# A two-layer block on one core: feed-forward gate and up with weights stationary, both parts of the tokens as 512 moving columns, and another order of weight tiles

## The reference

```python
D_MODEL = 2048; SEQ = 256; D_FF = 5632; FFN_CONV_WIDTH = 3

def causal_dwconv(u, w, b):      # K taps over positions, w[K-1] hits the current token
    up = jnp.pad(u, ((0, 0), (K - 1, 0), (0, 0)))
    return b + sum(up[:, k:k + S] * w[k] for k in range(K))

def conv_glu_ffn(h, w_gate, w_up, conv_w, conv_b, w_down):
    g = causal_dwconv(h @ w_gate, conv_w, conv_b)
    return (jax.nn.silu(g) * (h @ w_up)) @ w_down

h = rmsnorm(x, g_ffn[l]) * (1.0 + sc2) + sh2
x = x + gt2 * conv_glu_ffn(h, w_ffn_gate[l], w_ffn_up[l], ffn_conv_w[l], ffn_conv_b[l], w_ffn_down[l])
```

## Time and profile before

| | |
|---|---|
| median of 3 runs | 3034.95 us (3034.37 to 3036.27) |
| span of the profiled execution | 3033.7 us (no other time is given for it) |
| TensorE matmuls | 3020.3 us busy, 14581 instructions |
| TensorE weight loads (beside the matmuls) | 2537.3 us busy |
| VectorE, ScalarE | 1971.3 us, 1494.1 us busy |
| from memory | 658.21 MB, 217 GB/s in the mean |

### The profile page before, as it was taken

How to read it: one execution, slowest core, us unless ns; L and a number is a source line. 1 busy time by engine, 2 the same in 40 slices (tenths; PEclk the granted TensorE clock), 3 DMA queues, 4 the chain that set the end, 5 groups by cost and what they waited for, 6 DMA issues and landing times.

```text
span 3033.7 us, 38889 instructions
## 1 busy us (share of the span) xinstructions
PE 3020.3 (100%) x14581; PEld 2537.3 (84%) x14581; DVE 1971.3 (65%) x2081; ACT 1494.1 (49%) x1798; POOL 15.1 (0%) x32
## 2 busy tenths in 40 slices
PE   9999999999999999999999999999999999999999
PEld 7899878888888888888888888888888888888887
DVE  7999997866655568665555656565475555566564
ACT  6555456444444545554444444545454444444543
POOL 0000000000000000000000000000000000000000
PEclk9999999999999999999999999999999999999999
DMA  9998998865556556555555455555555555455555
GB/s 397 414 403 297 360 344 299 303 220 188 188 187 190 189 180 227 172 177 179 190 177 194 160 173 194 174 183 186 163 177 180 194 173 194 165 170 189 169 183 173
DMA packets 167272, 658.21 MB, mean 217 GB/s; under 512 B 18593, under 2 KB 18913, under 8 KB 154721
## 3 DMA queue, kind: packets, MB, share of 16 engines
q1 hardware_dynamic: 163264, 634.53, 60.6%
q0 software_dynamic: 3584, 21.48, 1.9%
q10 hardware_dynamic: 290, 0.33, 0.0%
HBM read 654.14 MB, written 2.11 MB: 216 GB/s over the span
## 4 chain that ended last, share of the span: by engine, by line
PE 91%; DVE 5%; DMA 3%; ACT 1%; issue 0%; SPq 0%; DVEq 0%; ACTq 0%
PE pg L1229 27%; PE pg L1231 27%; PE pg L1230 27%; DMA w_raw<-w 2%; DVE w_lo L1891 2%; PE pm L1264 1%; DVE R L1835 1%; PE pm L1292 1%; PE pm L1722 1%; DMA R<-w_ada 1%; PE pg L1315 1%; PE pg L1316 1%; PE pg L1317 1%; DVE x_rows L1835 1%; PE pm L1616 0%
## 5 line engine op out<-in xcount | busy, mean ns | idle before, releaser
L1771 DVE TENSOR_TENSOR w_lo<-w_raw,w_hi 128x1024 fp32r<-128x1024 f32 x868 | 1060.9, 1225 | 948.5 <-ACT w_hi L625 944.2
L625 ACT ACTIVATE w_hi<-w_raw 128x1024 fp32r<-128x1024 f32 x868 | 919.8, 1060 | 1295.6 <-PE pg L1231 1285.9
L1229 PE MATMUL pg<-w_hi,hT_hi 128*128 128x512 f32 x2912 | 1144.2, 393 | 1.0 <-DVE w_lo L1891 0.7
L1231 PE MATMUL pg<-w_hi,hT_lo 128*128 128x512 f32 x2912 | 1134.1, 389 | 0.0
L1230 PE MATMUL pg<-w_lo,hT_hi 128*128 128x512 f32 x2912 | 1133.5, 389 | 0.0
L1229 PEld LDWEIGHTS pg<-w_hi,hT_hi 128*128 128x128 f32 x2912 | 547.0, 188 | 114.4 <-issue 3.4
L1231 PEld LDWEIGHTS pg<-w_hi,hT_lo 128*128 128x128 f32 x2912 | 546.6, 188 | 114.5
L1230 PEld LDWEIGHTS pg<-w_lo,hT_hi 128*128 128x128 f32 x2912 | 547.1, 188 | 110.0
L1229 PE MATMUL pg<-w_hi,y_parts 128*128 128x512 f32 x864 | 337.6, 391 | 0.0
L1231 PE MATMUL pg<-w_hi,y_parts 128*128 128x512 f32 x864 | 336.4, 389 | 0.0
L1230 PE MATMUL pg<-w_lo,y_parts 128*128 128x512 f32 x864 | 336.1, 389 | 0.0
(11 more groups left out here) (321 smaller groups left out, 1957.4 us busy)
## 6 DMA issues: line engine op xcount, KB each, us to landing
w_raw<-w SPq DMA_DIRECT2D x1008, 512.0 KB, 4.1
R<-w_ada SPq DMA_DIRECT2D x59, 1024.0 KB, 8.6
x_rows<-w_ada SPq DMA_DIRECT2D x18, 1024.0 KB, 10.6
R<-w_ada POOLq DMA_DIRECT2D x11, 1024.0 KB, 7.9
R<-w SPq DMA_DIRECT2D x16, 512.0 KB, 9.4
R<-w_ada SPq DMA_DIRECT2D x10, 512.0 KB, 7.5
R<-mem_T SPq DMA_DIRECT2D x8, 512.0 KB, 9.2
x_rows<-x SPq DMA_DIRECT2D x4, 1024.0 KB, 9.3
```

The costliest lines, as they stand in the source:

```text
L625: act.activation(w_hi[:, g % RING, :, :].rearrange("p c n -> p (c n)"), raw[:, g % RING, :], ACT.Copy).then_inc(hi_done, 1)
L1229: pe.matmul(out, hi, w_hi[:, slot, c, :], start=start, stop=False)
L1231: return pe.matmul(out, lo, w_hi[:, slot, c, :], start=False, stop=stop)
L1771: tt(flat(w_lo[:, g % RING, :, :]), raw[:, g % RING, :], flat(w_hi[:, g % RING, :, :]).bitcast(F32), ALU.subtract).then_inc(lo_done, 1)
```

## The change

- Gate and up in the blocks: `both_parts` takes the place of `group`. 128 columns of a weight tile are stationary, and the result has channels on partitions, so that there is nothing to transpose. The high and the low part of the tokens lie in one tensor, `hT_parts`, and move side by side as 2 x 256 columns against the high weights; the low weights meet the high part alone, 256 columns, into the first half of the same bank. The four pieces of 128 channels fill the four banks of `pm`.
- The halves of each bank are added by VectorE in one reduction (`summed`), to `g_sum` or `u_sum`. The tap and the convolution read `g_sum`, the product reads `u_sum`. `take`, `g_tok`, `u_tok` and `ff_T` are gone.
- Order of tiles in a step: gate of j + 1 (8), the first two down pieces of j (4), up of j + 1 (8), the other two down pieces (4). The stream of weights is laid out accordingly.
- Gate and up of block 0, in the front, go by `column_passes`. ScalarE takes `g0` in four activations with the tap's bias and scale; `u0` is read from PSUM by VectorE. Tap, convolution and Silu of block j + 1 are made in step j.
- Each engine's order is written anew (`block_of` on VectorE). The 16 `weigh` pieces are spread over three blocks. The load of the final gain waits for `aT_ready` in place of `ff_ps`.

```diff
-COLUMNS = ("y", "q0", "x", "k0", "q1", "k1")
+COLUMNS = ("y", "q0", "x", "k0", "q1", "k1", "g0", "u0")
...
-F_ACTS = list(itertools.accumulate(int(not name.startswith("o")) for name in FRONT))
+F_ACTS = list(itertools.accumulate(int(not name.startswith("o") and name != "u0") for name in FRONT))
...
-        hT_hi = sb("hT_hi", [P, KD, S], F32R)
-        hT_lo = sb("hT_lo", [P, KD, S], F32R)
+        hT_parts = sb("hT_parts", [P, 2, KD, S], F32R)
+        hT_hi, hT_lo = hT_parts[:, 0, :, :], hT_parts[:, 1, :, :]
...
-        g_tok = view(24, TB, NW)
-        u_tok = view(28, TB, NW)
+        g_sum = view(24, 4, S)
+        u_sum = view(28, 4, S)
...
-                    pool.wait_ge(ff_ps, NFF * 4)
+                    pool.wait_ge(aT_ready, NFF)
...
-                        if name == "x":
+                        if name in ("x", "g0"):
+                            taps, w, bias = (4, "conv_w", "conv_b") if name == "x" else (3, "ffn_w", "ffn_b")
                             for b in range(4):
-                                i = act.activation(X_[:, b, :], front_bank(u)[:, b // 2, b % 2 * S:(b % 2 + 1) * S],
-                                                   ACT.Identity, bias=V("conv_b")[:, b:b + 1],
-                                                   scale=V("conv_w")[:, 4 * b + 3:4 * b + 4])
+                                i = act.activation(front_dest[name][:, b, :],
+                                                   front_bank(u)[:, b // 2, b % 2 * S:(b % 2 + 1) * S],
+                                                   ACT.Identity, bias=V(bias)[:, b:b + 1],
+                                                   scale=V(w)[:, taps * b + taps - 1:taps * b + taps])
...
-                for q in range(2):
-                    act.wait_ge(ff_ps, j * 4 + q + 1)
-                    for c in range(2):
-                        k = 2 * q + c
-                        i = act.activation(g_cv[:, k, :], pm[q][:, c * S:(c + 1) * S], ACT.Identity,
-                                           bias=ff_col("ffn_b", j, k, 1), scale=ff_col("ffn_w", j, k, 3, 2))
-                    i.then_inc(ff_tap, 1)
+                act.wait_ge(ff_summed, 2 * j)
+                for k in range(4):
+                    i = act.activation(g_cv[:, k, :], g_sum[:, k, :], ACT.Identity,
+                                       bias=ff_col("ffn_b", j, k, 1), scale=ff_col("ffn_w", j, k, 3, 2))
+                i.then_inc(ff_tap, 1)
...
+            silu(0)
             with act.Fori(0, NFF - 2) as j:
                 g0 = G_FF + 2 + j * 3
-                advance(g0)
-                tap(j)
-                act.wait_ge(ff_ps, j * 4 + 4)
-                take(g0, 0, flat(g_tok))
-                split(g0 + 1, range(4, 6))
-                silu(j)
-                split(g0 + 1, range(6, 8))
-                split(g0 + 2, range(4))
-                take(g0 + 1, 1, flat(u_tok))
-                advance(g0 + 2)
+                split(g0, range(4, 13))
+                tap(j + 1)
+                split(g0, range(13, 19))
+                silu(j + 1)
+                split(g0, range(19, 28))
...
+            split(g0, range(4, 13))
+            tap(j + 1)
+            split(g0, range(13, 14))
             act.wait_ge(y_ready, 2)
             gate_row(1)
-            split(g0 + 2, range(4, 6))
-            tap(NFF - 1)
-            split(g0 + 2, range(6, 8))
-            silu(NFF - 1)
-            split(g0 + 3, range(8))
+            split(g0, range(14, 19))
+            silu(j + 1)
+            split(g0, range(19, 32))
...
+            def both_parts(G, first):
+                for j in range(GT):
+                    g = first + j
+                    pe.wait_ge(lo_done, G * GT + g + 1)
+                    for c in range(KC):
+                        k = j * KC + c
+                        for b in range(4):
+                            hi, lo = (w[:, g % RING, c, b * P:(b + 1) * P] for w in (w_hi, w_lo))
+                            pe.matmul(pm[b].rearrange("p (a s) -> p a s", a=2), hi, hT_parts[:, :, k, :],
+                                      start=k == 0, stop=False)
+                            i = pe.matmul(pm[b][:, 0:S], lo, hT_hi[:, k, :], start=False, stop=k == KD - 1)
+                    i.then_inc(tile_used, 1)
...
-            def ff_T(j):
-                pe.wait_ge(evac_act, A_FF + j * 2 + 2)
-                transposes(g_tok, (0, 1), ff_ps)
-                transposes(u_tok, (2, 3), ff_ps)
...
+            def down(G, j, n, first, lhs, between=lambda i: None):
+                pe.wait_ge(evac_dve, V_FF + j * NB + n - 1)
+                short(G, first, n, lhs, between)
             with pe.Fori(0, NFF - 2) as j:
                 g0 = G_FF + 2 + j * 3
-                pe.wait_ge(evac_act, A_FF + j * 2 + 1)
-                pe.wait_ge(evac_dve, V_FF + j * NB - 1)
-                group(g0, 0, hT)
-                ff_T(j)
-                pe.wait_ge(evac_dve, V_FF + j * NB)
-                group(g0 + 1, 1, hT)
-                down(g0 + 2, j, A_FF + j * 2 + 4)
+                pe.wait_ge(ff_summed, 2 * j + 1)
+                both_parts(g0, 0)
+                pe.wait_ge(aT_ready, j + 1)
+                for n in range(2):
+                    down(g0, j, n, 8 + 2 * n, (aT_hi, aT_lo))
+                pe.wait_ge(ff_summed, 2 * j + 2)
+                both_parts(g0, 12)
+                for n in range(2, 4):
+                    down(g0, j, n, 16 + 2 * n, (aT_hi, aT_lo))
             j = NFF - 2
             g0 = G_FF + 2 + j * 3
-            pe.wait_ge(evac_act, A_FF + j * 2 + 1)
-            pe.wait_ge(evac_dve, V_FF + j * NB - 1)
-            group(g0, 0, hT)
-            ff_T(j)
-            pe.wait_ge(evac_dve, V_FF + j * NB)
-            group(g0 + 1, 1, hT)
+            pe.wait_ge(ff_summed, 2 * j + 1)
+            both_parts(g0, 0)
+            down(g0, j, 0, 8, (aT_hi, aT_lo))
+            pe.wait_ge(ff_summed, 2 * j + 2)
+            pe.wait_ge(ff_tap, j + 1)
             gate_row(1)
-            for n in range(NB):
-                pe.wait_ge(evac_dve, V_FF + j * NB + n - 1)
-                pe.wait_ge(evac_act, A_FF + j * 2 + (3 if n == 0 else 4))
-                short(g0 + 2, n, (aT_hi, aT_lo))
-                if n == 0:
-                    pe.wait_ge(gate_sb, 2)
-                    ff_T(NFF - 1)
+            down(g0, j, 1, 10, (aT_hi, aT_lo))
+            pe.wait_ge(gate_sb, 2)
+            both_parts(g0, 12)
+            for n in range(2, 4):
+                down(g0, j, n, 16 + 2 * n, (aT_hi, aT_lo))
...
+            def conv(j, k, src):
+                d = 2 - k
+                for m in range(4):
+                    w = vec[:, bass.ds(VEC["ffn_w"][0] + (j * 4 + m) * 3 + k, 1)]
+                    step(stt(g_cv[:, m, d:], src(m)[:, 0:S - d], w, g_cv[:, m, d:], ALU.mult, ALU.add))
+                step.settle()
+            def convolved(j, k):
+                if k == 1:
+                    dve.wait_ge(ff_tap, j)
+                conv(j, k, lambda m: g_sum[:, m, :])
+                if k == 0:
+                    dve.sem_inc(ff_conv, 1)
+            def summed(G, last, dest):
+                dve.wait_ge(tile_used, G * GT + last)
+                dve.tensor_reduce(out=dest, in_=pm_all[:, :, :].rearrange("p b (a s) -> p b s a", a=2), op=ALU.add,
+                                  axis=mybir.AxisListType.X).then_inc(ff_summed, 1)
+            def product(j):
                 dve.wait_ge(ff_silu, j + 1)
-                dve.wait_ge(ff_ps, j * 4 + 4)
-                for q in range(2):
-                    step(tt(flat(a_f[:, 2 * q:2 * q + 2, :]), flat(g_cv[:, 2 * q:2 * q + 2, :]), pm[2 + q][:, :],
-                            ALU.mult))
+                if isinstance(j, int) and j == 0:
+                    dve.wait_ge(tile_used, FT)
+                    for q in range(2):
+                        step(tt(flat(a_f[:, 2 * q:2 * q + 2, :]), flat(g_cv[:, 2 * q:2 * q + 2, :]), pg[1][:, q, :],
+                                ALU.mult))
+                else:
+                    u = u_sum
+                    dve.wait_ge(ff_summed, 2 * j + 1)
+                    step(tt(flat(a_f), flat(g_cv), flat(u), ALU.mult))
                 step.settle()
-                split_act(a_f, hi, lo, aT_ready)
-            def down_out(G, j, n):
-                dve.wait_ge(tile_used, G * GT + 2 * n + 2)
+            def product_high(hi):
+                step(dve.tensor_copy(hi, a_f))
...
+            def block_of(j, weighed=(), final=False):
                 g0 = G_FF + 2 + j * 3
+                def to(first, last):
+                    for g in range(first, last):
+                        split(g0, (g,))
+                        if g in weighed:
+                            weigh(next(gate_blocks))
+                to(4, 5)
                 product(j)
+                to(5, 6)
+                dve.wait_ge(tile_used, g0 * GT)
+                product_high(aT_hi)
+                to(6, 7)
+                product_low(aT_hi, aT_lo)
```

(37 more changed lines are left out.)

## The result

| | before | with the change |
|---|---|---|
| median of 21 runs | 3035.07 us (3033.06 to 3038.2) | 3039.39 us (3036.82 to 3042.41) |
| ratio | 1 | 1.0013, 95% interval 1.0007 to 1.0019 |
| span of the profiled execution | 3033.7 us | 3035.4 us (its time 3037.19) |

The change makes the kernel slower by 0.13%, 4.3 us (2.1 to 5.8 by the interval). The forecast was 3.8 us faster, in a range of 3022 to 3040 that the median is inside of. The sign was wrong.

What follows compares the result with a forecast made beforehand. TensorE's own sequence of matmuls was taken to bound the kernel. Terms -19.5 + 8.3 + 2.5 + 0.7 + 1.5 + 1.6 + 0.9 + 0.2 made -3.8 us: 3031 us, range 3022 to 3040.

Steps and rivals of the forecast that it cites:

- transposes and restarts: TensorE in the blocks: removing 176 transposes and the slow restarts behind them, 11 sets of 1.77 us, saves 19.5 us.
- gate and up in the blocks, 1280 pairs: TensorE, 160 tiles: 8 matmuls of 512 columns and 8 of 256 replace 12 of 512, adding 8.3 us.
- wait at the entry: TensorE before block 0's first group waits for VectorE's signal after a low part: +1.5 us with the cold restart.
- wait at the gate row: Last block: the gate row's transpose waits for the tap of block 10, +1.6 us (0.5 to 3.7).
- wait for down's bank: Last block: down of block 10 waits for the bank VectorE empties for n = 2, +0.9 us (0 to 3.0).
- the steady rates: TensorE's matmul prices inside long runs of one form: 0.2267 us for 512 columns, 0.1198 us for 256.
- Alternating is dear: Rival, chance 0.13: two-run operands or each change of form cost TensorE extra; at 0.354 us a pair, 3041 us.
- Short behind long is cheap: Rival, chance 0.20: each 256 behind a 512 costs 0.1135 us, a pair 0.340, 8.3 us go: 3023 us.
- the sums are slow: Rival, chance 0.14: VectorE's sums take 4.4 us each, the two last waits grow by 2.1 us each: 3036 us.
- the new waits are hidden: Rival, chance 0.10: the three new TensorE waits of 4.0 us fall away: 3027 us.
- The margin of block 0: First group in the blocks: VectorE's tile 4 is ready at 10.9 us, TensorE needs it at 12.6; holds by 1.7.
- the cover of the sums inside the blocks: Inner blocks: four down tiles (10.9 us) cover the sum ending at S + 4.9; TensorE waits 0 us.

Runs made afterwards that it cites:

- the four-transpose run: Kernel before with four of its sixteen transposes per block, the other twelve left out: 3022.1 us, ratio 0.9956 to before.
- the runs of four and of eight: Changed kernel with four or eight 512-column matmuls in a row, then as many of 256: 22.43 and 22.32 us a group; eight timed 3034.14 us, ratio 0.9994 to before.
- an unbroken row of 128: Changed kernel with the low weights also moving both token parts, so all gate and up matmuls have 512 columns: 3167.78 us.
- runs of sixteen: Changed kernel without its three TensorE waits, tiles alternately high-low and low-high, giving sixteen matmuls of one form in a row: 3028.57 us, ratio 0.9975 to before.
- the parts side by side: Changed kernel with the tokens' high and low parts adjacent in memory, one run of 512 columns: 22.60 us a group, 0.3531 a pair.

## Why the prediction was wrong, step by step

| term | predicted | measured |
|---|---|---|
| transposes and restarts | -19.5 | -19.5 by the period; the four-transpose run confirms the price of one |
| gate and up in the blocks, 1280 pairs | +8.3 (0 to +17.9) | +16.3: 19 groups of 22.60 and one of 22.2, less 160 x 12 x 0.2267 |
| gate and up of block 0 in the front | +2.5 | +2.0: 48.19 - 46.19 |
| down behind the shorter form | +0.7 | +0.4 to +0.6: 10.90 or 10.91 against 48 x 0.2267 = 10.88 |
| wait at the entry | +1.5 (1.3 to 2.6) | +1.6: 499.82 against 498.29, and the restart |
| wait at the gate row | +1.6 | +1.5 |
| wait for down's bank | +0.9 | +0.7 |
| restarts behind the two | +0.2 | +0.2 |
| sum | -3.8 | +3.3; the medians say +4.3 (2.1 to 5.8) |

The two traces give the same +3.3 us. From the first matmul of gate and up in the front (451.70 before, 450.10 after) to the second set of eight transposes of `x_rows`, in the last block, these two executions took 738.79 and 742.07 us:

```profile
1190.49 1.04 PE L1549 MATMUL pm<-con_sb,x_rows 128*128 128x128 f32 x8
```

```profile
1192.17 1.04 PE L1522 MATMUL pm<-con_sb,x_rows 128*128 128x128 f32 x8
```

**The step that failed** is "At steady rates, 8 x (0.2267 + 0.1198) - 12 x 0.2267 = +0.052 us; x 160 = +8.3 us", and with it "I take the steady rates, as they lie between the two". The mechanism (more matmuls, each with a fixed cost) was right and its term mis-sized: in 19 of 20 groups a pair costs 0.3531, not 0.3466, which makes the term +16.3 in place of +8.3 us, and these 8.0 us turn -3.8 into +4.2. The other terms came out 0.9 us lower together. The row that hinted at it was there. The 512s behind the 256s at 304.33 ran at 0.234 (0.232 by nanoseconds), and in a strict alternation every 512 stands behind a 256. The cheap 256 behind a 512 (0.1133), the other bound, is part of the same alternation too, and the pair was the sum 0.236 + 0.117. A middle between two bounds was taken where the new code repeats the one situation 1280 times. The middle was not an impossible price either: the first group ran at it. Had all 20 done so, by that group's rate, the time would have been some 8 us lower, near the forecast of 3031. No row of before could tell which of the two patterns the alternation would settle in.

**The rivals.** "Alternating is dear" is what happened, with 0.3531 for its 0.354, just short of its 3041 us. Of the two causes it named, the operand in two runs had no part, and a price for each change of form did not fit the runs of four and of eight either. Its chance of 0.13 was low, for the slow rows were direct evidence for it. "Short behind long is cheap", at 0.20, took one half of the alternation and left out the other. The sums took 2.29 us, as the line through the two reductions said, so "the sums are slow" fell. So did "the new waits are hidden": they showed at three places within 0.2 us of their worked-out lengths.

**What held.** The margin of block 0 (no wait of TensorE in its first group), the cover of the sums inside the blocks (no wait of TensorE in any inner block), and the signal at the entry. It left once VectorE's low part was issued (that one ran from 499.64 to 500.86, TensorE started at 499.82), the lower of its two bounds. The figure of the Trainium skill ("TensorE: Matmul & The Clock Gate", section "Wait — 56ns, not 53.3ns?"), 2.5 ns per warm matmul, would have made the whole +1.6 us for the pairs. The runs here do not agree with it: 512 columns cost 0.2266 us in an unbroken row of 128, 13 ns over their columns at the granted 2.4 GHz, and the term was +16.3 us.

## What to carry to other kernels

Where TensorE's own sequence is the bound, price a new order by the situation that it repeats, and look for the rows of that situation, here a long matmul behind a shorter one, instead of adding the steady rates of its parts. Put matmuls of one length together: the same 128 matmuls took 22.60 us by turns and 22.26 us in runs of sixteen. In runs of four and of eight, the first group, behind the stand, cost what the others did but for its slow first matmul. A term that rests on over a thousand small instructions needs its third digit, since 0.0065 us a pair (8 us in all) was more than all three stalls together (4 us). And look at every repetition: the first of 20 equal groups ran differently from the other 19.

## What the runs showed of the hardware that was not expected

- By turns with a 256, a 512-column matmul took 0.236 us in the mean (and the 256 0.117), and with runs of 4, 8 and 16 the pair was 0.3505, 0.3488 and 0.3478 us. The loss of a set of equal length grew with the run, from 0.007 to about 0.02 us, and in the runs of eight and sixteen it sat in the first five long ones behind the short ones.
- The same alternation ran at two prices. Behind a stand of 1.5 us, a whole group of 64 pairs took 0.3467 us a pair (in the change and with the parts side by side); entered from running matmuls, 0.3531 us in every group. With 384 columns in the short one it was the other way round, 0.413 behind the stand and 0.4064 else. What sets it is open.
- A pair of 512 and 448 columns (0.4375 us) lost more than one of 512 and 384 (0.4064) or 512 and 256 (0.3531): over their columns at 2.4 GHz 37.5, 33.1 and 33.1 ns, where two of 512 have 26.6.
- Whether the moving operand is one run of 512 or two of 256 that lie 16 KB apart made no difference of 0.01 us in 22.60.
- A bare signal on VectorE's queue did not wait for the instruction ahead of it to finish: TensorE started 1.04 us before that one ended.
